# Row ranks spread evenly over the partitions, and each expert's down projection as plain fp32 matmuls

## The chip, the cores and the metric

The kernel runs on one core of one Trainium2 chip. The metric is the device time of one execution in microseconds (us); lower is better. Three runs of the kernel before gave 1128.08, 1129.69 and 1132.62 us; the median is 1129.69 us.

## The reference

One layer of an encoder trunk on two sequences of 512 tokens with 1024 channels, in fp32. Its first two sub-layers (a mix of state-space heads, neighbourhood attention and pooling, then cross attention) are not touched. The third is a mixture of experts: each of the 1024 tokens picks one of four groups and then two of its eight experts, so the 32 experts get 64 rows each on average.

```
def expert_block(args):
    idx, wts, e = args
    xb = x_pad[idx]
    hb = jax.nn.silu(xb @ w_e_gate[e]) * (xb @ w_e_up[e])
    return (hb @ w_e_down[e]).astype(jnp.float32) * wts[:, None]
```

`w_e_gate` and `w_e_up` are 1024x256 for an expert, `w_e_down` is 256x1024, so an expert has three matrices of 1 MiB each.

## The kernel before

**Order of the work.** A written-out list of steps (`timeline()`) orders everything up to the router. Then comes a loop over the 32 experts, which takes the last 370 us or so. Each engine has its own program, and semaphores couple them.

**Splitting in two.** The matrix products are made from fp32 operands split into a high part (an fp32r copy made by ACT) and a low part (the difference, made by DVE). `three` (lines 944 to 948) issues high*high, high*low and low*high as three fp32r matmuls. For the experts `ghi`/`egl` are the parts of the gate and up matrices, `xgH`/`xgL` those of the gathered rows.

**The expert's loop.** SP loads the matrices (`load_piece`, L891) into four buffers each, in the order gate and up of expert n, down of expert n-1; `load_in(n)` waits until expert n-4 has used its buffer (`g_used`), and `load_down` for `d_used`. POOL gathers the rows of an expert by an index list from HBM (`gather_rows`, into `xg`), gathers the partial sums of the same rows (`gather_sums`, into `pg`), and scatters the new sums back (`store_rows`), all with indirect copies of 4 KiB rows; a `gather_sums` waits until an earlier store into its buffer's place has landed (`px_st`). PE does, for n: turn the hidden rows of n-1 (`turn_hidden`), turn the rows of n+1 (`turn_rows`), gate and up of n (`gate_up`), and the down product of n-1 (`down`). ACT does `hidden_high(n-1)`, `rows_high(n+1)`, `gate_high(n+1)`, `hidden_silu(n)`, `down_high(n+1)`; DVE does `hidden_low(n-1)`, `rows_low(n+1)`, `gate_low(n+1)`, `hidden(n)`, `add_rows(n-1)`, `down_low(n+1)`. ACT and DVE take their instructions strictly in that order.

**The down product** contracts over 256 hidden channels, in two chunks k of 128. Before, chunk 0 is done with `three` from split operands (`hbH`, `hbL`, `dhi`, `edl`), chunk 1 as one plain fp32 matmul of `hbF` with the loaded matrix, for each of two halves of 512 columns.

**Where a row sits.** A token has a rank within its expert. `iota_s` holds for each of the 128 partitions the rank that it serves; a one-hot comparison with it (L2089) and a matmul give the list `idh` of the row for each partition. Partition p serves rank p//8 + 16*(p mod 8). Partitions whose rank is beyond the expert's count get an index out of bounds, and the copies skip them.

**The end.** When the first 28 experts' stores have landed, SP copies all partial sums to the outputs (L926, eight copies of 512 KB). Then POOL scatters the rows of the last four experts over them (`out_rows`, L2443).

Of the kernel before, what the change touches and what calls it, by code (L numbers as in the profile page):

```python
# [13 lines left out]
F32 = mybir.dt.float32  # L14
# [5 lines left out]
ALU = mybir.AluOpType  # L20
# [3 lines left out]
P = 128  # L24
# [5 lines left out]
NT = SEQS * TPS  # L30
# [13 lines left out]
NG, EPG, NE = 4, 8, 32  # L44
# [255 lines left out]
def encoder_layer(nc, dram, out):  # L300
# [3 lines left out]
    with ctx:  # L304
        def sem(name):
            return ctx.enter_context(nc.semaphore(name))
# [6 lines left out]
        hb_ps = ctx.enter_context(nc.psum_tensor("hb_ps", [P, 512], F32))  # L313
        r_ps = ctx.enter_context(nc.psum_tensor("r_ps", [P, 512], F32))
        y_ps = ctx.enter_context(nc.psum_tensor("y_ps", [P, 1024], F32))
# [142 lines left out]
        iota_s = sb("iota_s", [P, P])  # L458
# [34 lines left out]
        edr = [se(f"edr{i}", [P, 2, D], b, o) for i, (b, o) in enumerate(d_place)]  # L493
        edl = [se(f"edl{i}", [P, 2, D], b, o, F32R) for i, (b, o) in enumerate(d_place)]
        ghi = [se(f"ghi{i}", [P, 2, KT, DE], "x_sb", 4 * K4 * i, F32R) for i in range(2)]
        dhi = [se("dhi0", [P, 2, D], "Wl1", 0, F32R), se("dhi1", [P, 1, D], "Wl1", K4, F32R)]
# [6 lines left out]
        def sw(name, shape, dt=F32):  # L503
            t = nc.alloc_sbuf_tensor_at(name, shape, dt, offset=small[0])
            small[0] += -(-int(np.prod(shape[1:])) * (2 if dt == BF16 else 4) // 32) * 32
            assert small[0] <= at["router_b"]
            return t
# [2 lines left out]
        ehb = sw("ehb", [P, DE])  # L510
        hbH = sw("hbH", [P, 2, P], F32R)
        hbL = sw("hbL", [P, 2, P], F32R)
        hbF = sw("hbF", [P, P])
        idh = sw("idh", [P, NE], U32)
        idp = sw("idp", [P, NE], U32)
        ids = sw("ids", [P, NE], U32)
# [29 lines left out]
        r_pool = sem("r_pool")  # L546
# [12 lines left out]
        eg_ld = [[sem(f"eg_ld{i}{a}") for a in range(2)] for i in range(4)]  # L559
        ed_ld = [sem(f"ed_ld{i}") for i in range(4)]  # L560
        ghi_done = sem("ghi_done")
        dhi_done = sem("dhi_done")
        glo_done = sem("glo_done")
        dlo_done = sem("dlo_done")
        g_used = sem("g_used")
        d_used = sem("d_used")
        xg_ld = [sem(f"xg_ld{i}") for i in range(3)]
# [5 lines left out]
        hb_done = sem("hb_done")  # L573
        hb_full = sem("hb_full")
        hb_high = sem("hb_high")
        hb_low = sem("hb_low")
        ey_done = sem("ey_done")
        px_st = [sem(f"px_st{i}") for i in range(4)]
        copied = sem("copied")
# [90 lines left out]
        def wait_full(eng, step, j=0):  # L670

            n = plan.place[step, j]
            eng.wait_ge(full[n % N_BANKS], n // N_BANKS + 1)
# [269 lines left out]
        def _(pe):  # L943
            def three(dst, ah, al, bh, bl, first, last):

                pe.matmul(dst, ah, bh, start=first, stop=False)  # L946
                pe.matmul(dst, ah, bl, start=False, stop=False)  # L947
                return pe.matmul(dst, al, bh, start=False, stop=last)  # L948
# [51 lines left out]
            for step in TL:  # L1000
# [5 lines left out]
                if kind == "hT":  # L1006
# [6 lines left out]
                    for half in range(2):  # L1013
                        b = take(pe, step, half)
# [9 lines left out]
                elif kind == "hn3":  # L1024

                    pe.wait_ge(hnorm, 1 + nth(*step))
                    b = take(pe, step)
# [8 lines left out]
                elif kind == "dtt":  # L1036
                    wait_released(pe, ("dtp", step[1]))
                    b = take(pe, step)
# [4 lines left out]
                elif kind == "vt":  # L1043
                    wait_released(pe, ("vc",) + step[1:])
                    b = take(pe, step)
# [265 lines left out]
            def turn_hidden(n):  # L1311

                pe.wait_ge(hb_done, n + 1)
                if n:
                    pe.wait_ge(hb_low, n)
                for k in range(2):
                    last = pe.transpose(hb_ps[:, k * P:(k + 1) * P], ehb[:, k:DE:2], ident[:, :])
                last.then_inc(hb_full, 1)

            def down(n):  # L1320

                pe.wait_ge(hb_low, n + 1)
                pe.wait_ge(dlo_done, n + 1)
                if n:
                    pe.wait_ge(ey_done, n)
                lo = edl[n % 4]
                for half in range(2):
                    c = slice(half * 512, half * 512 + 512)
                    three(y_ps[:, c], hbH[:, 0, :], hbL[:, 0, :], dhi[n % 2][:, 0, c], lo[:, 0, c], True, False)
                    last = pe.matmul(y_ps[:, c], hbF[:, :], edr[n % 4][:, 1, c], start=False, stop=True)  # L1330
                last.then_inc(d_used, 1)

            turn_rows(0)
# [53 lines left out]
        def _(act):  # L1387
# [11 lines left out]
            def copy(dst, src, **kw):  # L1399
                return act.activation(dst, src, ACT.Copy, **kw)  # L1400
# [225 lines left out]
                    copy(xgH[n % 2][:, 4 * half:4 * half + 4, :],  # L1626
                         xg_ps[:, half * 512:half * 512 + 512].rearrange("p (a b) -> p a b", a=4)).then_inc(xg_high, 1)

            def down_high(n):
                act.wait_ge(ed_ld[n % 4], 16 * (n // 4 + 1))  # L1630
                if n > 1:
                    act.wait_ge(d_used, n - 1)
                elif n == 0:
                    wait_full(act, ("xo", NT - 1), 1)
                copy(dhi[n % 2][:, 0, :], edr[n % 4][:, 0, :]).then_inc(dhi_done, 1)

            def hidden_silu(n):
                act.wait_ge(g_used, n + 1)
                if n:
# [3 lines left out]
            def hidden_high(n):  # L1643
                act.wait_ge(hb_full, n + 1)
                if n:
                    act.wait_ge(d_used, n)
                copy(hbF[:, :], hb_ps[:, P:2 * P])
                copy(hbH[:, 0, :], hb_ps[:, 0:P]).then_inc(hb_high, 1)

            down_high(0)  # L1650
            act.wait_ge(ids_done, 1)
            act.wait_ge(g_in, 1)
            act.activation(r_g[:, :, :], r_g[:, :, :], ACT.Exp)
# [3 lines left out]
            gate_high(1, 1)  # L1657
            hidden_silu(0)
            rows_high(1)
            down_high(1)  # L1660
            for n in range(1, NE):
                hidden_high(n - 1)
                if n + 1 < NE:
                    rows_high(n + 1)
                    gate_high(n + 1, 0)
                    gate_high(n + 1, 1)
                hidden_silu(n)
                if n + 1 < NE:
                    down_high(n + 1)
            hidden_high(NE - 1)  # L1670

            def more_first():
                act.wait_ge(g_used, NE)
                act.wait_ge(hb_low, NE)

            def more(b):
                act.wait_ge(d_used, b + NE)
# [15 lines left out]
        def _(dve):  # L1693
# [424 lines left out]
                    tt(xgL[n % 2][:, f, :], xg_ps[:, half * 512:half * 512 + 512].rearrange("p (a b) -> p a b", a=4),  # L2118
                       xgH[n % 2][:, f, :].bitcast(F32), ALU.subtract).then_inc(xg_low, 1)

            def down_low(n):
                dve.wait_ge(dhi_done, n + 1)
                tt(edl[n % 4][:, 0, :], edr[n % 4][:, 0, :], dhi[n % 2][:, 0, :].bitcast(F32), ALU.subtract)\  # L2123
                    .then_inc(dlo_done, 1)

            def hidden(n):
                dve.wait_ge(th_done, n + 1)
                if n:
                    dve.wait_ge(hb_full, n)
                b = gu_ps[n % 2]  # L2130
                tt(ehb[:, :], eth[:, :], b[:, DE:2 * DE], ALU.mult).then_inc(hb_done, 1)

            def hidden_low(n):
                dve.wait_ge(hb_high, n + 1)
                tt(hbL[:, 0, :], hb_ps[:, 0:P], hbH[:, 0, :].bitcast(F32), ALU.subtract).then_inc(hb_low, 1)

            def add_rows(n):
                e = expert(n)
# [52 lines left out]
                dve.tensor_copy(ovi[:, NO:NO + 1], ov[:, 1, NE - 1:NE]).then_inc(count_done, 1)  # L2191

            gate_low(0, 1)
            down_low(0)
            rows_low(0)
            gate_low(1, 0)
            gate_values()
# [1 line left out]
            gate_low(1, 1)  # L2199
            rows_low(1)  # L2200
            slot_values()
            down_low(1)
            for n in range(1, NE):
                hidden_low(n - 1)
                if n + 1 < NE:
                    rows_low(n + 1)
                    gate_low(n + 1, 0)
                    gate_low(n + 1, 1)
                hidden(n)
                add_rows(n - 1)  # L2210
                if n + 1 < NE:
                    down_low(n + 1)
                if n == 2:
                    counts()
                if n == 3:
                    half_rows()
            hidden_low(NE - 1)
            add_rows(NE - 1)

            def more_first():  # L2220
# [65 lines left out]
        def _(pool):  # L2286
# [25 lines left out]
            for step in TL:  # L2312
# [7 lines left out]
                elif kind == "gain":  # L2320
# [5 lines left out]
                    if step[1] == "ffn":  # L2326
                        pool.memset(router_w[:, :, NG:8], 0.0)
                        pool.memset(router_b[:, NG:8], NEG).then_inc(r_pool, 1)
                        pool.iota(iota_e[:, :], [[1, NE]], base=0, channel_multiplier=0,
                                  allow_small_or_imprecise_dtypes=True).then_inc(r_pool, 1)  # L2330
                        pool.iota(iota_p[:, :], [[1, P]], base=0, channel_multiplier=0,
                                  allow_small_or_imprecise_dtypes=True).then_inc(r_pool, 1)
                        pool.iota(iota_s[:, :].rearrange("p (a b) -> p a b", a=16), [[1, 16], [16, 8]], base=0,
                                  channel_multiplier=0, allow_small_or_imprecise_dtypes=True).then_inc(r_pool, 1)
                        pool.iota(token0[:, :], [[P, NT]], base=0, channel_multiplier=1,
                                  allow_small_or_imprecise_dtypes=True).then_inc(r_pool, 1)
                        pool.iota(token1[:, :], [[P, NT]], base=1, channel_multiplier=1,
                                  allow_small_or_imprecise_dtypes=True).then_inc(r_pool, 1)
                        parts = (("w_router_group", "b_router_group", 0, NG), ("w_router_expert", "b_router_expert", 8, NE))
                        for w, b_, o, m in parts:  # L2340
                            pool.dma_start(router_w[:, :, o:o + m], dram[w][0].rearrange("(k p) n -> p k n", p=P))\
                                .then_inc(router_ld, 16)
                            pool.dma_start(router_b[:, o:o + m], bass.AP(dram[b_].tensor, 0, [[0, P], [1, m]]))\
                                .then_inc(router_ld, 16)
# [232 lines left out]
```

## Time and profile before

| | |
|---|---|
| median of three runs | 1129.69 us |
| the profiled execution, its own time | 1130.85 us |
| its span in the profile | 1129.0 us |
| PE busy over the span | 1002.6 us (89%) |
| DVE / ACT / POOL busy | 774.9 / 474.0 / 299.7 us |
| moved by DMA in all | 197.41 MB |
| mean granted TensorE clock | 0.948 |

The profile shows one execution. A window's row gives its bounds and length, the busy time of PE, of PE's weight loads, DVE, ACT and POOL in it (with the number of instructions), then the granted clock of TensorE (1.00 is full speed), the mean busy share of the core's 16 DMA engines, and the rate they moved. A matmul's duration includes its fill and drain, which overlap with the next matmul; the chain of waits counts only the time by which each one moved the chain on. "L1330" is line 1330 of the kernel.

### The profile page before, as it was taken

The page shows a single profiled execution, that of the slowest core. Times are in us where ns is not written, and L with a number is a line of the kernel's source. Part 1 is how long each engine was busy: PE and PEld are TensorE (multiplying, and loading weights), DVE is VectorE, ACT ScalarE, POOL GpSimd, SP SyncE. Part 2 cuts the span into 40 slices and gives each one's busy share as a digit, 9 for nine tenths or more (in the row PEclk, how much of TensorE's full clock was granted, in tenths as well). Part 3 has the DMA queues.
Part 4 walks back from the last instruction along what each step waited for, and adds up shares of the span by engine and source line. Part 5 has one row for each costly group of instructions (what it writes and reads, how often), then busy time and mean ns, then how long its engine had stood idle before and what let it go on. Part 6 is the DMA issues. An engine that isn't in the chain of part 4 may idle for free.

```text
span 1129.0 us, 13999 instructions
## 1 busy us (share of the span) xinstructions
PE 1002.6 (89%) x5029; PEld 801.8 (71%) x5029; DVE 774.9 (69%) x1241; ACT 474.0 (42%) x860; POOL 299.7 (27%) x347
## 2 busy tenths in 40 slices
PE   5998988998989899999979999849999988888892
PEld 4776767776768678788868888737777766666671
DVE  5557677776777577862455777668988877787771
ACT  5144442233455234322233343325666655555540
POOL 2234132312521422100110212023354332323122
PEclk9999998997999989899989999958999999999996
DMA  7222242111223514424120112937999999999872
GB/s 237 84 85 94 66 142 76 57 56 56 94 75 98 163 58 136 129 71 178 56 63 19 57 57 109 376 135 272 360 363 369 378 362 342 362 336 368 329 251 74
DMA packets 63396, 197.41 MB, mean 175 GB/s; under 512 B 16416, under 2 KB 22976, under 8 KB 50912
## 3 DMA queue, kind: packets, MB, share of 16 engines
q1 hardware_dynamic: 43344, 152.73, 37.4%
q0 software_dynamic: 18688, 39.52, 10.0%
q10 hardware_dynamic: 1296, 4.26, 0.9%
q8 instruction: 41, 0.67, 0.2%
q14 instruction: 27, 0.22, 0.1%
HBM read 190.17 MB, written 37.75 MB: 202 GB/s over the span
## 4 chain that ended last, share of the span: by engine, by line
PE 51%; DMA 18%; DVE 13%; issue 9%; ACT 4%; POOL 3%; SPq 0%; ACTq 0%; POOLq 0%; DVEq 0%
PE bank L946 10%; PE bank L947 9%; PE bank L948 9%; DMA partial_rows<-pg,idh 9%; DMA edr<-w_e_down 4%; PE gu_ps L946 2%; PE gu_ps L948 2%; PE gu_ps L947 2%; PE bank L1017 2%; PE bank L1135 2%; PE y_ps L1330 2%; DMA pg<-partial_rows,idh 2%; DVE egl L1740 1%; DVE Wl L1758 1%; ACT dec L1585 1%
## 5 line engine op out<-in xcount | busy, mean ns | idle before, releaser
L946 PE MATMUL bank<-Wh,hTh 128*128 128x512 f32 x384 | 156.6, 408 | 1.2 <-DVE hTl L1782 1.2
L1740 DVE TENSOR_TENSOR egl<-egr,ghi 128x2048 fp32r<-128x2048 f32 x64 | 143.9, 2288 | 15.0 <-ACT ghi L1400 15.0
L947 PE MATMUL bank<-Wl,hTh 128*128 128x512 f32 x384 | 152.1, 396 | 0.0
L948 PE MATMUL bank<-Wh,hTl 128*128 128x512 f32 x384 | 151.6, 395 | 0.0
L1400 ACT ACTIVATE ghi<-egr 128x2048 fp32r<-128x2048 f32 x64 | 119.6, 1931 | 0.0
L946 PE MATMUL gu_ps<-ghi,xgH 128*128 128x512 f32 x256 | 104.0, 406 | 1.4 <-DVE xgL L2118 1.4
L948 PE MATMUL gu_ps<-ghi,xgL 128*128 128x512 f32 x256 | 101.2, 395 | 0.0
L947 PE MATMUL gu_ps<-egl,xgH 128*128 128x512 f32 x256 | 100.9, 394 | 0.0
L946 PEld LDWEIGHTS bank<-Wh,hTh 128*128 128x128 f32 x384 | 74.0, 193 | 17.8 <-issue 1.6
L1400 ACT ACTIVATE dhi<-edr 128x1024 fp32r<-128x1024 f32 x32 | 33.9, 1060 | 122.9 <-DMA edr<-w_e_down 93.2
L948 PEld LDWEIGHTS bank<-Wh,hTl 128*128 128x128 f32 x384 | 73.6, 192 | 16.2
L947 PEld LDWEIGHTS bank<-Wl,hTh 128*128 128x128 f32 x384 | 73.9, 193 | 14.6
L2438 POOL DMA_INDIRECT pg<-partial_rows,idh x32 | 43.2, 1351 | 146.0 <-DMA partial_rows<-pg,idh 142.9
L946 PE MATMUL bank<-hTh,Wh 128*128 128x512 f32 (+1 forms) x176 | 73.3, 416 | 1.1 <-DVE x_sb L1818 0.8
L947 PE MATMUL bank<-hTl,Wh 128*128 128x512 f32 (+1 forms) x176 | 70.9, 403 | 0.0
L948 PE MATMUL bank<-hTh,Wl 128*128 128x512 f32 (+1 forms) x176 | 70.6, 401 | 0.0
L1330 PE MATMUL y_ps<-edr,hbF 128*128 128x512 f32 x128 | 65.4, 592 | 0.0
L2123 DVE TENSOR_TENSOR edl<-edr,dhi 128x1024 fp32r<-128x1024 f32 x32 | 39.1, 1221 | 38.3 <-ACT dhi L1400 38.3
L1758 DVE TENSOR_TENSOR Wl<-raw,Wh 128x1024 fp32r<-128x1024 f32 (+1 forms) x45 | 55.0, 1228 | 12.3 <-ACT Wh L1400 12.3
L2297 POOL TENSOR_SCALAR ms<-ssq 128x1 f32<-128x1 f32 x28 | 6.4, 230 | 212.0 <-ACT xn_ffn L1460 96.8
L1585 ACT ACTIVATE dec<-dec,ncs 128x128 f32<-128x128 f32 x128 | 38.3, 388 | 50.8 <-DVE dec L1961 50.8
L946 PEld LDWEIGHTS gu_ps<-ghi,xgH 128*128 128x128 f32 x256 | 49.1, 192 | 11.0 <-DVE xgL L2118 1.8
(326 smaller groups left out, 2231.7 us busy)
## 6 DMA issues: line engine op xcount, KB each, us to landing
egr<-w_e_gate SPq DMA_DIRECT2D x32, 1024.0 KB
egr<-w_e_up SPq DMA_DIRECT2D x32, 1024.0 KB
edr<-w_e_down SPq DMA_DIRECT2D x32, 1024.0 KB
raw<-w_in SPq DMA_DIRECT2D x50, 256.0 KB, 3.0
xn<-w_in SPq DMA_DIRECT2D x22, 256.0 KB, 3.0
x_sb<-x_prompt SPq DMA_DIRECT2D x8, 512.0 KB, 6.5
partial_rows<-x_sb ACTq DMA_DIRECT2D x8, 512.0 KB, 2.6
ffn_rows<-xn_ffn POOLq DMA_DIRECT2D x8, 512.0 KB, 3.0
```

The costliest lines, as they stand in the source:

```text
L946: pe.matmul(dst, ah, bh, start=first, stop=False)
L947: pe.matmul(dst, ah, bl, start=False, stop=False)
L948: return pe.matmul(dst, al, bh, start=False, stop=last)
L1017: last = pe.transpose(b[:, j * P:(j + 1) * P], src[:, f * P:(f + 1) * P], ident[:, :])
L1135: last = pe.matmul(b[:, hc], dec[:, dr, h, :], xdt[:, dr, hc], start=dr == 0, stop=dr == 1)
L1330: last = pe.matmul(y_ps[:, c], hbF[:, :], edr[n % 4][:, 1, c], start=False, stop=True)
L1400: return act.activation(dst, src, ACT.Copy, **kw)
L1585: last = act.activation(dec[:, dr, h, :], dec[:, dr, h, :], ACT.Exp, bias=ncs[:, dr, c, h:h + 1])
L1740: tt(egl[n % 4][:, a, :, :], egr[n % 4][:, a, :, :], ghi[n % 2][:, a, :, :].bitcast(F32), ALU.subtract)\
L1758: tt(lo, src, h, ALU.subtract).then_inc(w_low, 1)
L2123: tt(edl[n % 4][:, 0, :], edr[n % 4][:, 0, :], dhi[n % 2][:, 0, :].bitcast(F32), ALU.subtract)\
L2438: return pool.indirect_dma_start(out=to, out_offset=None, in_=table, in_offset=bass.IndirectOffsetOnAxis(ap=idx, axis=0), bounds_check=bou ...
```

## The change

Two things. First, `iota_s` gets another pattern: partition p = 16a + 8b + 4c + d serves rank 2a + 16b + c + 32d (a below 8, b and c below 2, d below 4). Second, both chunks of the down product become plain fp32 matmuls of the loaded matrix with the hidden rows; the split of the down matrix (`down_high` on ACT, `down_low` on DVE) and the low part of the hidden rows (`hidden_low` on DVE) go, and one ACT copy of 256 columns takes the place of two of 128. PE waits directly for the load of the down matrix.

```diff
-        hbF = sw("hbF", [P, P])
+        hbF = sw("hbF", [P, 2, P])
...
             def down(n):
-                pe.wait_ge(hb_low, n + 1)
-                pe.wait_ge(dlo_done, n + 1)
+                pe.wait_ge(hb_high, n + 1)
+                pe.wait_ge(ed_ld[n % 4], 16 * (n // 4 + 1))
                 if n:
                     pe.wait_ge(ey_done, n)
-                lo = edl[n % 4]
                 for half in range(2):
                     c = slice(half * 512, half * 512 + 512)
-                    three(y_ps[:, c], hbH[:, 0, :], hbL[:, 0, :], dhi[n % 2][:, 0, c], lo[:, 0, c], True, False)
-                    last = pe.matmul(y_ps[:, c], hbF[:, :], edr[n % 4][:, 1, c], start=False, stop=True)
+                    for k in range(2):
+                        last = pe.matmul(y_ps[:, c], hbF[:, k, :], edr[n % 4][:, k, c], start=k == 0, stop=k == 1)
...
-            def down_high(n):
-                act.wait_ge(ed_ld[n % 4], 16 * (n // 4 + 1))
-                if n > 1:
-                    act.wait_ge(d_used, n - 1)
-                elif n == 0:
-                    wait_full(act, ("xo", NT - 1), 1)
-                copy(dhi[n % 2][:, 0, :], edr[n % 4][:, 0, :]).then_inc(dhi_done, 1)
...
-                copy(hbF[:, :], hb_ps[:, P:2 * P])
-                copy(hbH[:, 0, :], hb_ps[:, 0:P]).then_inc(hb_high, 1)
+                copy(hbF[:, :, :], hb_ps[:, 0:2 * P].rearrange("p (a b) -> p a b", a=2)).then_inc(hb_high, 1)
...
-            def down_low(n):
-                dve.wait_ge(dhi_done, n + 1)
-                tt(edl[n % 4][:, 0, :], edr[n % 4][:, 0, :], dhi[n % 2][:, 0, :].bitcast(F32), ALU.subtract)\
-                    .then_inc(dlo_done, 1)
...
-            def hidden_low(n):
-                dve.wait_ge(hb_high, n + 1)
-                tt(hbL[:, 0, :], hb_ps[:, 0:P], hbH[:, 0, :].bitcast(F32), ALU.subtract).then_inc(hb_low, 1)
...
-                        pool.iota(iota_s[:, :].rearrange("p (a b) -> p a b", a=16), [[1, 16], [16, 8]], base=0,
-                                  channel_multiplier=0, allow_small_or_imprecise_dtypes=True).then_inc(r_pool, 1)
+                        pool.iota(iota_s[:, :].rearrange("p (a b c d) -> p a b c d", a=8, b=2, c=2),
+                                  [[2, 8], [16, 2], [1, 2], [32, 4]], base=0, channel_multiplier=0, allow_small_or_imprecise_dtypes=True).then_inc(r_pool, 1)
```

The calls of the removed functions go too, and waits on `hb_low` elsewhere become waits on `hb_high` or `d_used`.

## Rows read from the trace of the kernel before

**Rows 1.** Windows: PE, PEld, DVE, ACT, POOL busy, clock, DMA share, GB/s

```profile
784.00:889.00 105.00, 104.49 (x476) 80.98 (x475) 93.50 (x97) 69.66 (x87) 48.64 (x31) 1.00 0.97 372
900.00:1080.00 180.00, 158.67 (x701) 118.28 (x700) 138.03 (x129) 99.60 (x129) 53.39 (x46) 1.00 0.91 347
```

**Rows 2.** Timeline of SP's queue: loads issued as gate_up of an expert ends

```profile
781.58 0.33 SPq L891 DMA_DIRECT2D egr<-w_e_gate  x1
...
821.24 0.33 SPq L891 DMA_DIRECT2D egr<-w_e_gate  x1
...
889.28 0.33 SPq L891 DMA_DIRECT2D egr<-w_e_gate  x1
...
899.02 0.33 SPq L891 DMA_DIRECT2D egr<-w_e_gate  x1
...
1057.16 0.33 SPq L891 DMA_DIRECT2D egr<-w_e_gate  x1
```

**Rows 3.** Waits between 760 and 1080 us: total, times, longest in us

```profile
POOL pg L2438 <- DMA partial_rows<-pg,idh: 130.0, 20, 8.2
ACT dhi L1400 <- DMA edr<-w_e_down: 88.3, 18, 5.6
```

**Rows 4.** The chain that ended last, around one down product

```profile
1057.12 0.23 PE y_ps L946
...
1057.82 0.86 PE y_ps L1330 x2
...
1059.38 0.87 PE y_ps L1330 x2
1060.27 25.60 DMA edr<-w_e_down
```

**Rows 5.** Windows in which DMA carries little but indirect row copies

```profile
761.00:762.00 1.00, 0.90 (x2) 0.80 (x3) 0.05 (x1) 1.00 (x1) 0.70 (x2) 0.50 0.58 213
...
766.00:767.00 1.00, 1.00 (x5) 0.86 (x4) 0.90 (x4) 0.00 (x0) 0.00 (x0) 0.86 0.48 70
```

**Rows 6.** Windows: a plain store of 128 rows alone, and matrix loads alone

```profile
646.00:647.00 1.00, 1.00 (x11) 0.96 (x9) 0.71 (x3) 0.00 (x0) 0.00 (x0) 1.00 0.97 401
...
718.00:722.00 4.00, 4.00 (x33) 3.66 (x31) 3.72 (x15) 0.38 (x3) 0.79 (x3) 1.00 1.03 432
```

**Rows 7.** Groups of instructions by form, 720 to 1129 us

```profile
L1330 PE MATMUL y_ps<-edr,hbF 128*128 128x512 f32 x128 | 65.4, 592 | 0.0
...
L2123 DVE TENSOR_TENSOR edl<-edr,dhi 128x1024 fp32r<-128x1024 f32 x32 | 39.1, 1221 | 38.3 <-ACT dhi L1400 38.3
L1400 ACT ACTIVATE dhi<-edr 128x1024 fp32r<-128x1024 f32 x32 | 33.9, 1060 | 122.9 <-DMA edr<-w_e_down 93.2 <-PE y_ps L1330 29.7
...
L1641 ACT ACTIVATE eth<-gu_ps 128x256 f32<-128x256 f32 x32 | 12.6, 393 | 17.4 <-PE gu_ps L948 17.4
```

**Rows 8.** Timeline: POOL around the table, and an indirect copy beside another

```profile
560.61 0.37 POOL L2333 IOTA iota_s<- 128x128 f32 x1
...
760.60 1.00 POOL L2438 DMA_INDIRECT pg<-partial_rows,idh  x1 [0.31 <-issue]
...
761.90 1.00 POOL L2438 DMA_INDIRECT pg<-partial_rows,idh  x1 [0.30 <-issue]
```

**Rows 9.** Timeline of the end

```profile
1073.15 1.28 DVE L2143 SCALAR_TENSOR_TENSOR pg<-y_ps,gate_s,pg 128x1024 f32<-128x1024 f32 x1
...
1090.01 2.50 SPq L926 DMA_DIRECT2D y_prompt<-partial_rows  x4
...
1100.98 0.38 ACT L1641 ACTIVATE eth<-gu_ps 128x256 f32<-128x256 f32 x1 [5.02 <-PE gu_ps L948]
...
1107.17 1.01 POOL L2443 DMA_INDIRECT y_prompt<-pg,idp  x1 [13.90 <-issue]
...
1109.05 1.28 DVE L2143 SCALAR_TENSOR_TENSOR pg<-y_ps,gate_s,pg 128x1024 f32<-128x1024 f32 x1 [3.48 <-PE y_ps L1330]
...
1114.89 0.97 POOL L2443 DMA_INDIRECT y_prompt<-pg,idp  x1 [0.30 <-issue]
```

More of the change, by code:

```diff
@@ L561, in encoder_layer @@
         ghi_done = sem("ghi_done")
-        dhi_done = sem("dhi_done")
         glo_done = sem("glo_done")
-        dlo_done = sem("dlo_done")
         g_used = sem("g_used")
@@ L575, in encoder_layer @@
         hb_high = sem("hb_high")
-        hb_low = sem("hb_low")
         ey_done = sem("ey_done")
@@ L1314, in turn_hidden @@
                 if n:
-                    pe.wait_ge(hb_low, n)
+                    pe.wait_ge(hb_high, n)
                 for k in range(2):
@@ L1646, in hidden_high @@
                     act.wait_ge(d_used, n)
-                copy(hbF[:, :], hb_ps[:, P:2 * P])
-                copy(hbH[:, 0, :], hb_ps[:, 0:P]).then_inc(hb_high, 1)
-            down_high(0)
+                copy(hbF[:, :, :], hb_ps[:, 0:2 * P].rearrange("p (a b) -> p a b", a=2)).then_inc(hb_high, 1)
             act.wait_ge(ids_done, 1)
@@ L1659, in _ @@
             rows_high(1)
-            down_high(1)
             for n in range(1, NE):
@@ L1667, in _ @@
                 hidden_silu(n)
-                if n + 1 < NE:
-                    down_high(n + 1)
             hidden_high(NE - 1)
@@ L1673, in more_first @@
                 act.wait_ge(g_used, NE)
-                act.wait_ge(hb_low, NE)
+                act.wait_ge(d_used, NE)
             def more(b):
@@ L2193, in _ @@
             gate_low(0, 1)
-            down_low(0)
             rows_low(0)
@@ L2201, in _ @@
             slot_values()
-            down_low(1)
             for n in range(1, NE):
-                hidden_low(n - 1)
                 if n + 1 < NE:
@@ L2210, in _ @@
                 add_rows(n - 1)
-                if n + 1 < NE:
-                    down_low(n + 1)
                 if n == 2:
@@ L2216, in _ @@
                     half_rows()
-            hidden_low(NE - 1)
             add_rows(NE - 1)
```

## The prediction

> **What bounds the kernel now.** I read the windows by stage first, then SP's queue, the waits and the chain. The change touches only the expert loop, so everything before 781 us stays (the table itself is one instruction on POOL of 0.37 us at 560 us [rows 8], far from its use).
>
> The loop has two halves. Until 889 us PE is busy 104.5 of 105 us; from 900 to 1080 us it is busy 158.7 of 180 us, with the DMA engines busy 0.91 of the time at 347 GB/s [rows 1]. SP's queue gives the pace, since it issues a gate matrix whenever the product gate_up of an expert ends: the rows at 781.58 and 821.24 us are experts 1 and 5, those at 889.28, 899.02 and 1057.16 us experts 12, 13 and 27. From 821.24 to 889.28 us that is 68.04/7 = 9.72 us an expert; from 899.02 to 1057.16 us it is 158.14/14 = 11.30 us [rows 2]. So PE paces the first twelve experts and DMA the rest: PE at first lives on the matrices loaded ahead. Drawn backwards at 11.30 us an expert from 899.02 us, DMA's line stands at 763.4 us for expert 1, which is 18.2 us ahead of PE's 781.58; that is the lead. The waits agree: ACT stands 88.3 us for down matrices and POOL 130.0 us for stores of partial sums to land [rows 3], and the chain goes through a down load of 25.60 us [rows 4].
>
> **Why DMA needs 11.30 us.** An expert moves 3 x 1 MiB of matrices and 3 x 64 rows of 4 KiB (rows in, sums in, sums out), 3.15 + 0.79 = 3.93 MB; 347 GB/s x 11.30 us = 3.92 MB agrees. But when DMA has little but indirect row copies, it stands at a share of 0.48 to 0.58 and at most some 210 GB/s [rows 5], while a plain store of 128 rows of the same size reaches 0.97 and 401 GB/s, and matrices alone 432 GB/s [rows 6]. The old table puts ranks 0 to 63 on the partitions with p mod 8 below 4: four used, four unused, all along. I read this as: the DMA engines serve fixed small blocks of partitions, and half of them get nearly all rows. Check: the loaded half carries 3.15/16 + 0.79/8 = 0.295 MB per engine and expert; at one engine's rate of 383/16 = 23.9 GB/s (372 at 0.97 [rows 1] is 383 at full share) to 432/16 = 27.0 GB/s that is 12.3 to 10.9 us, which brackets 11.30. Against it: were all rows on eight engines, the mean share would be (1 + 0.197/0.295)/2 = 0.83, not 0.91, so some rows (ranks above 63) lie on the others.
>
> **The table.** With the new one, ranks 0 to 63 take two partitions in every block of four, so every engine carries 0.246 MB: 10.3 us at 23.9 GB/s, 9.1 us at 27.0. The share gives the same upper end: 0.91 x 11.30 = 10.3 us. I take 10.2, near the mixed row. It costs nothing.
>
> **The down product on PE.** One chunk split in three moves the chain by 0.23 us three times, 0.69 us (one of three rows stands), one plain fp32 chunk (two instructions) by 0.86 to 0.87 [rows 4]. For both halves: before 2 x (0.69 + 0.865) = 3.11 us, after 4 x 0.865 = 3.46. So PE pays 0.35 us more for each expert, and its pace becomes 10.07 us. The lower bound is that the saved changes between kinds of matmul give the 0.35 back (9.72); the upper takes the mean duration of one L1330 instruction, 592 ns [rows 7], as if none overlapped: 8 x 0.592 = 4.74 us, a pace of 11.35. I take 0.865 because it is the distance of starts in the chain, while 592 ns contains the wait behind the neighbour.
>
> The page "FP8 and Floating Point Precision" of the Trainium skill, section TensorE Precision Notes, has true fp32 as four passes through the array. Four times the 0.23 us of an fp32r pass [rows 4] would be 0.92, where the row has 0.865; by the rule the down product would be 3.68 us and the pace 10.29 us, 7 us more over the loop.
>
> **ACT and DVE.** ACT loses 1.06 us (dhi) an expert, and for two copies of 128 columns it gets one of 256, 0.39 us by the silu of that width. DVE loses the 1.22 us of edl [rows 7] and the small subtraction for hbL. While PE paces, both are partly hidden already (DVE 93.5 of 105 us, ACT 69.7 [rows 1]); I count nothing for them. They hide behind PE's 10.07 us, DVE had 93.5/105 x 9.72 = 8.7 us of work in it and has less now. What does count is the place of a wait. ACT stood at `down_high(n+1)` for a down load, with `hidden_high(n)`, `rows_high(n+2)` and `gate_high(n+2)` queued behind it, although gate and up of n+2 had been loaded before that down matrix. Now PE waits for the down matrix of n only after gate_up of n+1, one expert later. Where DMA paces, the gate split starts up to one load earlier: 1.05 MB at 347 GB/s = 3 us, once, plus the 1.06 us. Where PE paces, nothing. POOL: its `gather_sums` waits for stores, and behind it are queued `store_rows` and `gather_rows`; with half the rows per loaded engine those land sooner, and nothing new is waited for.
>
> **The sum.** PE's line: expert 1 at 781.6 us, 30 experts x 10.07 = 302.1, less 0.9 for the last one, which turns no rows: the last gate_up ends at 1082.8 instead of 1100.98 us [rows 9]. DMA's line: 763.4 + 30 x 10.2 = 1069.4 us, 13 us ahead, so PE paces to the end; DMA would take over only above 10.64 us an expert. That is -18.2 us at the last gate_up.
>
> The end has two paths [rows 9]. PE's: down of 30, turn, copy, down of 31 and the addition end 9.4 us later (before 9.35: 1110.33 - 1100.98), at 1092.2; the last scatters start no earlier, and from the one at 1114.89 to the span's end at 1129.0 are 14.1 us: 1106.3. The stores': the addition for expert 27 ended at 1074.43 us, 54.6 us before the end (15.6 until the stores had landed and SP copied at 1090.01, 17.2 for the copies, 21.8 for scatters and landing). Now it ends at 781.6 + 27 x 10.07 + 4.7 = 1058.2, so the span ends at 1112.8 if stores land as slowly as before, and at 1106.3 (PE's path) if they land in half the time. I take 1111. This path is the likelier, since the copies follow the slowest store. The profiled execution took 1.85 us more than its span and 1.16 more than the median, so the median becomes 1111 + 1.85 - 1.16 = 1111.7, say 1112.
>
> **Rivals.**
> (B) DMA gains only part and paces the last experts. For it: mixed windows never show more than 383 GB/s at full share. Against: rows and matrices alone both exceed 400. At 10.95 us an expert its line ends at 763.4 + 328.5 = 1091.9 us, 9 us behind PE's line; less up to 4 us for the earlier split: 1117 to 1121. The page "DMA: Bandwidth & Descriptors" of the Trainium skill, section Where 436 GB/s comes from, says that for HBM traffic a limit of some 358 GB/s per core binds. By that, 3.93 MB would take 10.97 us and this rival would come true at its slow end. Matrices alone at 432 GB/s [rows 6] speak against the rule here, so it gets a small part of this case.
> (C) The table does nothing. The half share of the indirect copies may be POOL's pace: one copy each 1.30 us [rows 8], and 64 rows in 1.30 us are 202 GB/s, just what the windows show. Against: after the last of them the engines still work on at 0.48 [rows 5], and 11.30 us fits the loaded half. Then DMA keeps 11.30 us, its line ends where it does now, only the earlier down wait gives 0 to 4 us: 1125 to 1130.
> (D) Slower: plain fp32 costs PE what the 592 ns say. Pace 11.35 us: the last gate_up at 781.6 + 340.5 - 0.9 = 1121.2 us, 20 us late: 1150. It decides from the point where PE's pace passes 10.68 us, that is 0.51 us an instruction instead of 0.43; there the last gate_up ends where it does now. The chain's rows speak against it.
>
> **Chances.** Forecast 0.60 (1106 to 1117); B 0.17; C 0.15; D 0.05; faster still, below 1105, 0.03. A measurement of this kernel can tell about 0.5% from no change, 5.6 us: faster means below 1124.0, slower above 1135.3. So faster 0.60 + 0.17 + 0.03 = 0.80, same 0.14 of C, slower D with the rest, 0.06. Range: 1105 to 1124 leaves out C, D and the fastest tail, 0.2.
>
> **What would show it.** Right: loads of gate matrices in SP's queue every 10.07 us up to the last expert, PE busy near 100% to the end of the loop, DMA at 385 to 395 GB/s, copies of rows alone at a share near 1.0, eight L1330 instructions taking 3.46 us in a row, and stores landing within some 10 us. Wrong: a pace above 10.7 us late in the loop with PE idle (B, C); row copies alone still at a share of 0.55 (C); L1330 instructions starting 0.5 us or more apart (D). The prediction also fails if DMA's share was held up by something other than the rows.

## The result, and the profile after

The changed kernel takes 1104.86 us (median of four runs, 1101.08 to 1105.81) against 1130.38 us for the kernel before: a ratio of 0.9768, with a 95% interval of 0.9737 to 0.9799. It is faster by about 25.5 us, where 18 were forecast; the forecast of 1112 us was 7 us too slow, and the measured median lies 0.14 us below the stated range. The profiled execution is the fastest of the four, 1101.08 us with a span of 1099.3 us. It came to the list of rows (`idh`) 4.1 us earlier than the profiled one of before, at 748.56 instead of 752.68 us, before any line of the change matters. Its own time stands 3.8 us below the median, and the span difference of 29.7 us flatters the change.

Windows of the changed kernel, in the columns of [rows 1]:

```profile
784.00:889.00 105.00, 105.00 (x438) 74.10 (x437) 78.24 (x74) 55.34 (x62) 46.71 (x30) 1.00 0.99 381
889.00:1000.00 111.00, 111.00 (x468) 79.19 (x467) 81.85 (x67) 60.38 (x67) 50.34 (x33) 1.00 1.00 395
```

PE is busy every microsecond in both; before, it was idle for 21 of the 180 us in the second stretch [rows 1]. The DMA engines move 395 GB/s where they moved 347. DVE has 78.2 us of work where it had 93.5.

SP's queue, as in [rows 2]: each row is the end of gate_up of an expert, here 1, 2, 26 and 27.

```profile
774.41 0.33 SPq L888 DMA_DIRECT2D egr<-w_e_gate  x1
...
784.46 0.33 SPq L888 DMA_DIRECT2D egr<-w_e_gate  x1
...
1025.63 0.33 SPq L888 DMA_DIRECT2D egr<-w_e_gate  x1
...
1035.68 0.33 SPq L888 DMA_DIRECT2D egr<-w_e_gate  x1
```

The first and last are 26 experts apart: 261.27/26 = 10.05 us, and the pairs at both ends have the same 10.05. There is no second half any more. The down product is one piece of the chain:

```profile
1055.74 3.43 PE y_ps L1326 x8
```

Eight instructions in 3.43 us, 0.43 each, although the group of L1326 still gives a mean of 592 ns. The waits between 760 and 1060 us have turned round. Of the two waits of [rows 3], that of 130.0 us has shrunk to 1.7 us and that of 88.3 us is gone:

```profile
POOL partial_rows L2411 <- DVE pg L2117: 145.2, 28, 9.3
ACT hbF L1396 <- PE hb_ps L1314: 95.4, 30, 3.3
...
POOL pg L2406 <- DMA partial_rows<-pg,idh: 1.7, 1, 1.7
```

POOL and ACT now wait for what PE drives, no longer for DMA. The stretch before the loop, where DMA carries little but row copies (compare [rows 5]):

```profile
755.00:756.00 1.00, 0.00 (x0) 0.00 (x0) 0.80 (x2) 1.00 (x2) 0.82 (x1) 0.50 0.74 246
756.00:757.00 1.00, 0.98 (x2) 0.83 (x3) 0.00 (x0) 1.00 (x2) 0.69 (x2) 0.50 0.76 246
757.00:758.00 1.00, 1.00 (x4) 0.77 (x3) 0.91 (x1) 1.00 (x2) 0.69 (x2) 0.50 0.77 242
...
759.00:760.00 1.00, 1.00 (x5) 0.77 (x5) 0.90 (x5) 1.00 (x1) 1.00 (x1) 0.83 0.64 242
```

In the first three rows the share is 0.74 to 0.77, well above the 0.48 to 0.58 of before, but not the 1.0 that the prediction wanted to see.

And the end, as in [rows 9]:

```profile
1054.89 2.50 SPq L923 DMA_DIRECT2D y_prompt<-partial_rows  x4
```

```profile
1071.89 1.01 POOL L2411 DMA_INDIRECT y_prompt<-pg,idp  x1 [13.69 <-issue]
...
1079.98 0.97 POOL L2411 DMA_INDIRECT y_prompt<-pg,idp  x1 [3.22 <-DVE pg L2117]
...
1085.12 0.97 POOL L2411 DMA_INDIRECT y_prompt<-pg,idp  x1 [2.89 <-DVE pg L2117]
```

The addition for expert 27 ended at 1050.45 us, and SP could copy 4.4 us later instead of 15.6. POOL's last two pairs of scatters waited for DVE's additions, that is for PE's last products. Before, all eight went out one behind the other, since the stores had been late.

### The profile page after: what moved, and what is told of

Its sections match the earlier page's. It is cut to its first block, busy times and chain, and to the rows that moved or that the text cites. A ratio compares the mean times of both kernels' runs of the same rounds, so it can differ in the third digit from the quotient of the medians.

```text
span 1099.3 us, 13712 instructions
## 1 busy us (share of the span) xinstructions
PE 1003.5 (91%) x4965; PEld 787.2 (72%) x4965; DVE 734.9 (67%) x1177; ACT 446.7 (41%) x796; POOL 315.4 (29%) x347
## 4 chain that ended last, share of the span: by engine, by line
PE 69%; DVE 12%; issue 8%; ACT 3%; POOL 3%; DMA 2%; SPq 0%; ACTq 0%; POOLq 0%; DVEq 0%
PE bank L943 10%; PE bank L944 10%; PE bank L945 10%; PE y_ps L1326 9%; PE gu_ps L943 5%; PE gu_ps L945 5%; PE gu_ps L944 5%; PE xg_ps L1292 3%; PE bank L1014 2%; PE bank L1132 2%; DVE Wl L1741 1%; ACT dec L1581 1%; PE bank L1219 1%; PE bank L1263 1%; PE bank L1187 1%
## 5 line engine op out<-in xcount | busy, mean ns | idle before, releaser
L1326 PE MATMUL y_ps<-edr,hbF 128*128 128x512 f32 x256 | 115.1, 592 | 1.2 <-DVE pg L2117 1.2
L1326 PEld LDWEIGHTS y_ps<-edr,hbF 128*128 128x128 f32 x256 | 48.5, 190 | 49.9 <-issue 45.9
L2406 POOL DMA_INDIRECT pg<-partial_rows,idh x32 | 75.4, 2356 | 11.2 <-issue 9.5
L2117 DVE SCALAR_TENSOR_TENSOR pg<-y_ps,gate_s,pg 128x1024 f32<-128x1024 f32 x32 | 41.1, 1284 | 53.4 <-PE y_ps L1326 51.8
L2411 POOL DMA_INDIRECT partial_rows<-pg,idh x28 | 28.3, 1009 | 145.2 <-DVE pg L2117 145.2
## 6 DMA issues: line engine op xcount, KB each, us to landing
egr<-w_e_up SPq DMA_DIRECT2D x32, 1024.0 KB, 10.2
edr<-w_e_down SPq DMA_DIRECT2D x32, 1024.0 KB, 10.2
```

Source lines behind the costliest of these rows:

```text
L1326: last = pe.matmul(y_ps[:, c], hbF[:, k, :], edr[n % 4][:, k, c], start=k == 0, stop=k == 1)
L2117: stt(pg[n % 4][:, :], y_ps[:, :], gate_s[:, e:e + 1], pg[n % 4][:, :], ALU.mult, ALU.add)\
L2406: return pool.indirect_dma_start(out=to, out_offset=None, in_=table, in_offset=bass.IndirectOffsetOnAxis(ap=idx, axis=0), bounds_check=bou ...
L2411: return pool.indirect_dma_start(out=table, out_offset=bass.IndirectOffsetOnAxis(ap=idx, axis=0), in_=frm, in_offset=None, bounds_check=bo ...
```

## The experiments

The kernel before was measured anew beside them, at 1129.21 us for e1 to e4 and 1130.68 us for e5, e6, e8 and e9; each ratio is to its own one of these.

**One part alone.** The first kernel is the kernel before with the new table only; the second is the changed kernel with the old table.

```diff
 e1 (on the kernel before), the reverse for e2 (on the changed kernel):
-  pool.iota(iota_s[:, :].rearrange("p (a b) -> p a b", a=16), [[1, 16], [16, 8]], ...)
+  pool.iota(iota_s[:, :].rearrange("p (a b c d) -> p a b c d", a=8, b=2, c=2),
+            [[2, 8], [16, 2], [1, 2], [32, 4]], ...)
```

> The kernel before with the new rank table alone; the down product stays split. Theory (the table frees DMA, the plain down product costs PE 0.35 us an expert): PE paces to the end at 9.72 us an expert instead of 10.05, DMA follows at about 9.95 us (3.93 MB at 395 GB/s) within its lead of some 18 us; time 1130 - 26 - 10 = 1094 us. Rival 1 (ACT's wait for the down matrix, which stays here, holds up the gate split as soon as DMA is near its limit): pace above 10 us late in the loop, ACT again idle for tens of us before L1400 dhi, time 1100 to 1108. Rival 2 (the gain came from the down product, not from the table): about 1130.

Measured: 1094.17 us (1092.93 to 1095.71), a ratio to the kernel before of 0.9682 (0.9661 to 0.9704). That is the theory's number. The loop runs at 9.72 us an expert to the end, but for one step of 10.51 us after gate_up of expert 3 that the kernel before has too; SP's rows of experts 1, 2 and 27:

```profile
778.59 0.33 SPq L891 DMA_DIRECT2D egr<-w_e_gate  x1
...
788.31 0.33 SPq L891 DMA_DIRECT2D egr<-w_e_gate  x1
...
1032.12 0.33 SPq L891 DMA_DIRECT2D egr<-w_e_gate  x1
```

ACT's wait for the down load is harmless as soon as DMA keeps up: in this run's list of waits `dhi` waits 80.8 us for PE's down products, and no wait for a down load appears among the longest. Rivals 1 and 2 fall. The table alone beats the whole change by 10.7 us in the medians (1104.86 - 1094.17). Against the kernel before of its own series it saves 35.0 us where the whole change saves 25.5, which makes 9.5; the profiled executions differ by 9.5 too, from the list of rows to the end (550.7 and 541.2 us).

> The changed kernel with the old rank table. Theory: DMA paces the late experts at 11.2 to 11.3 us again, since half of its engines carry the rows; only the later wait for the down matrix helps, once and by 0 to 4 us: 1125 to 1130 us, PE idle in the second half, indirect copies alone at a DMA share of 0.5 to 0.6. Rival (fewer ACT and DVE instructions and the later wait are what freed the loop): pace of 10.05 us to the end and about 1105 us.

Measured: 1129.41 us (1127.22 to 1132.47), ratio 1.0004 (0.9989 to 1.0020). The down product gives nothing by itself, as forecast. But the loop is not what it was. Gate_up of experts 1 and 19 end at 779.56 and 960.44 us, 10.05 us an expert, and only then comes DMA's pace, 11.3 us on average (970.91 us for expert 20, 1072.38 us for expert 29). The last gate_up ends at 1092.44 instead of 1100.98 us, and still the end does not move, because the stores set it:

```profile
1088.46 2.50 SPq L923 DMA_DIRECT2D y_prompt<-partial_rows  x4
```

This is only 1.6 us earlier than in the kernel before [rows 9], 18.3 us after the addition for expert 27. The path of the stores, not PE's, ends the kernel here as it does before.

**Which partitions share an engine.** Two more tables tell two readings apart.

```diff
 e3 (on the kernel before, in place of the old pattern):
+  pool.iota(iota_s[:, :].rearrange("p (a b c d) -> p a b c d", a=2, b=2, c=8),
+            [[8, 2], [64, 2], [1, 8], [16, 4]], ...)
 e4 (on the changed kernel, in place of the new pattern):
+  pool.iota(iota_s[:, :], [[1, P]], ...)
```

> The kernel before with a third table: ranks 0 to 15 each in another group of partitions, rank r at partition 64*(r mod 16 // 8) + 4*(r mod 8) + r//16 (plus 28 from rank 64 on), so ranks 0 to 63 fill the partitions 0 to 31 and 64 to 95. Theory A (an engine serves a block of four partitions and the block 32 further on, and the upper 64 partitions have other engines): all engines are loaded evenly, as e1 or 0 to 2 us less: 1092 to 1094 us. Theory B (an engine serves every sixteenth block of four, so blocks 64 partitions apart share one): ranks 0 to 63 lie on half the engines again, and it ends like before, about 1130 us.

Measured: 1094.27 us (1093.28 to 1096.06), ratio 0.9691 (0.9668 to 0.9715).

> The changed kernel with rank r at partition r, so ranks 0 to 63 fill partitions 0 to 63. Theory A of e3: half of the engines carry nearly all rows, as with the old table: 1122 to 1130 us and a pace of 11.2 us late in the loop. Theory B: all 16 engines are loaded evenly, about 1105 us. A third reading (any dense packing is as good as the new table, only the old one's gaps hurt): 1105 us as well.

Measured: 1136.15 us (1134.99 to 1139.10), ratio 1.0057 (1.0040 to 1.0075). Both go with theory A and against B. Partitions 0 to 63 alone are half of the engines; 0 to 31 with 64 to 95 are all of them. The page "DMA: Bandwidth & Descriptors" of the Trainium skill, section The descriptor swizzle, gives for a plain transfer to 128 partitions the engine as 8*(partition >> 6) + ((partition >> 2) & 7). The old table, the new one, e3 and e4 all come out as that rule would have it for indirect copies.

The traces' records of single packets show the halves more directly. Take the five microseconds from 0.5 us after the first gather into `pg`, when little but rows is under way. Exactly eight packets of 4 KiB are in flight, as eight busy engines would have it, for 37% of that time in the kernel before and 34% in e4, but for 5% in the changed kernel and in e3. Twelve or more are in flight for 30% and 27% against 59% and 63%.

The straight table was expected at 1122 to 1130 us and is 6 us worse than that, and 6.7 us worse than e2. By the same rule an expert with 48 rows would put eight rows on some engines and four on others with the straight table, and six on each of its eight engines with the old one; that this is the reason was argued, not tried.

**What DMA can do by itself.** With the change PE paces the loop, so its trace can't show DMA's own limit. Three kernels take work from PE: they leave out the product of the rows' high part with the low part of the gate and up matrices.

```diff
 gate_up, in e5 (new table), e6 (old table) and e9 (table of e3):
-                    last = three(gu_ps[n % 2]..., xgH, xgL, hi, lo, k == 0, k == KT - 1)
...
+                    pe.matmul(g, xgH[n % 2][:, k, :], hi[:, :, k, :], start=k == 0, stop=False)
+                    last = pe.matmul(g, xgL[n % 2][:, k, :], hi[:, :, k, :], start=False, stop=k == KT - 1)
```

> The changed kernel (new table) with the low part of the gate and up matrices left out of gate_up: two matmuls for each k instead of three, so PE needs 8 x 0.227 = 1.8 us less for an expert (10.05 to 8.23 us) and is no longer what paces the loop. It leaves out one of the three products of gate and up. Theory: DMA paces at what 3.93 MB take at 395 GB/s, 9.9 to 10.0 us an expert, at a share of 1.00. Rival (DMA has more to give, the 395 GB/s in the changed kernel were only PE's demand): 9.2 to 9.5 us. In both cases the stage cannot go below DVE's 7.5 us.

Measured: 1087.16 us (two runs, 1087.05 and 1087.28), ratio 0.9614 (0.9594 to 0.9635). Not what was expected at first: experts 2 to 22 run at 8.85 us, not paced by DMA, since the lead lasts that long (and not at 8.23, so something beside PE's work holds it, which was not looked into). Then gate_up of experts 22 and 30 end at 962.65 and 1041.86 us: 9.90 us an expert, the theory's number. The two ends, and DMA in a stretch that holds the end of the lead and the start of its own pace:

```profile
962.65 0.38 ACT L1630 ACTIVATE eth<-gu_ps 128x256 f32<-128x256 f32 x1
...
1041.86 0.38 ACT L1630 ACTIVATE eth<-gu_ps 128x256 f32<-128x256 f32 x1
```

```profile
880.00:1000.00 120.00, 111.02 (x446) 72.94 (x445) 93.42 (x77) 69.95 (x79) 55.22 (x37) 1.00 1.02 419
```

> As e5, with the old table: the same product left out. Theory: DMA's own pace with half of its engines carrying the rows, 11.2 to 11.4 us an expert from the first experts on, at a share of 0.91 to 0.92; the loop ends where DMA's line ends in the kernel before, 1120 to 1130 us. Rival (PE's work also slows the DMA side of the kernel before): clearly below 11 us.

Measured: 1126.89 us (1125.55 to 1130.17), ratio 0.9969 (0.9955 to 0.9983). From expert 10 (859.37 us) to expert 30 (1083.61 us) the pace is 11.21 us. The late pace holds; "from the first experts on" does not, the lead carries nine experts here. Taking 1.8 us of PE's work out of each expert leaves the kernel with the old table 0.3% below the kernel before: DMA was the bound, whatever PE did.

```profile
880.00:1000.00 120.00, 97.47 (x359) 62.41 (x357) 77.26 (x64) 57.55 (x64) 50.39 (x33) 0.94 0.91 350
```

> As e5, with the table of e3, which spreads every 16 ranks over 16 groups of partitions where the new table needs 32 ranks for an even spread: the same product left out. Theory: the most loaded engine carries up to one row less of each copy, some 0.15 us each and 0.2 to 0.4 us an expert: 9.6 to 9.8 us. Rival (the limit is the sum over all engines, not the most loaded one): the same as e5 to 0.1 us.

Measured: 1080.63 us (two runs, 1080.13 and 1081.12), ratio 0.9557 (0.9535 to 0.9578), 6.5 us faster than e5. In the profiled executions 4.6 us of it lie between the list of rows and the last gate_up (294.5 against 299.2 us). At the end of its lead, from expert 25 (988.42 us) to expert 30 (1036.48 us), the pace is 9.61 us. With this table every 16 ranks are spread over all engines, so no engine gets two rows more than another. That fits the theory that the most loaded engine counts and not the sum over all, which would have left the pace at 9.9; the 9.61 rest on five experts of one execution.

**The place of the wait.** In e2 the last gate_up ended 8.5 us early where the prediction gave the later wait 0 to 4 us.

```diff
 e8 (on e2), ACT's loop:
                 hidden_silu(n)
+                if n + 1 < NE:
+                    act.wait_ge(ed_ld[(n + 1) % 4], 16 * ((n + 1) // 4 + 1))
```

> The kernel of e2 (old table, plain down product) with only the old wait put back: ACT waits for the down matrix of expert n+1 after the silu of n, without copying it. In e2 the last gate_up ended at 1092.4 us, 8.5 us before that of the kernel before, where 0 to 4 us were expected of the later wait. Theory (the place of the wait makes this): the last gate_up ends at 1098 to 1101 us. Rival (the removed copy and subtraction make it): it stays at 1092 to 1094 us. The whole time is set by the stores of partial sums and moves by less than half of that: 1129 to 1133 us.

Measured: 1129.21 us, ratio 0.9987 (0.9974 to 1.0000), and the wait is back:

```profile
ACT hbF L1396 <- DMA edr<-w_e_down: 84.5, 15, 7.5
```

DMA's pace sets in after expert 14, as it did after expert 13 in the kernel before and after expert 19 in e2. The last gate_up ends at 1096.14 us, between theory and rival. The three executions came to the list of rows at different times, so the distance from there is fairer: 348.3 us in the kernel before, 346.2 here, 341.8 in e2. So of 6.5 us the wait's place makes 4.4; the rest is the removed work, or differences between single executions. None of it reaches the end.

## Why the prediction was nearly right

**What bounds the kernel: right.** Rows on half of the engines, a lead used up by PE, then DMA's pace. e2 and e6 show 11.3 and 11.2 us with the old table, with PE's whole load and with less, e5 9.90 with the new one, where the prediction's term was 10.2 (9.1 to 10.3).

**PE's price: right.** 0.35 us an expert, measured 10.05 - 9.72 = 0.33, and some 10 us in all between e1 and the changed kernel. The 592 ns of a single instruction, on which rival D stood, were overlap. The page "FP8 and Floating Point Precision" of the Trainium skill, section TensorE Precision Notes, has four passes for true fp32, from which the prediction estimated 3.68 us for the product. The row is 3.43 us, so the estimate is 7% too high.

**ACT and DVE at nothing: right** for the time. Together with PE's price this makes the down part of the change a loss of some 10 us where PE paces, hidden in a change that gains 25. With the old table it costs nothing (e2).

**Why 7 us too slow.** Two terms were mis-sized. The first is the step "The change touches only the expert loop, so everything before 781 us stays". The distance from the list of rows to the end of gate_up of expert 1 is 28.90 us in the kernel before, 28.88 in e2, 28.93 in e4 and 29.5 in e8 (tables on half of the engines), but 25.86 in the changed kernel, 25.86 in e1 and 25.97 in e3: 3.0 us, and it goes with the table, not with the down product. One microsecond is PE's wait for the first gathered rows, 4.71 us instead of 5.67. The rest comes with TensorE's clock, in two parts. In the changed kernel the granted clock rose from 1.2 to 2.4 GHz at 759.3 us (the 0.83 in the row from 759 us shown above), 3.3 us into gate_up of expert 0; in the kernel before at 766.3 us, 5.2 us into it. That product took 7.3 us instead of 8.2. In all ten traces this rise comes 10.5 to 10.8 us after the list of rows with an even table and 13.5 to 14.5 us after it with the others. The other part comes one expert later. Windows of the kernel before and, below, of the changed one, each around the turning of expert 2's rows:

```profile
773.00:778.00 5.00, 4.34 (x18) 3.91 (x19) 3.78 (x8) 2.96 (x4) 1.18 (x2) 0.66 1.03 430
```

```profile
764.00:768.00 4.00, 1.48 (x23) 1.30 (x23) 3.96 (x6) 1.27 (x3) 2.80 (x1) 1.00 0.86 317
768.00:774.00 6.00, 6.00 (x32) 5.06 (x32) 4.03 (x5) 4.70 (x4) 1.00 (x1) 1.00 0.98 405
```

In both PE waits 2.52 us for DVE before it turns these rows. In the kernel before, the granted clock then fell for part of the stretch to its lower level of 1.2 GHz; in the changed one it stayed at 2.4. That makes gate_up of expert 1 end 11.06 instead of 12.30 us after that of expert 0. The table as such does not decide this part. The clock fell here in every kernel with a table on half of the engines (e6 too, 0.50 from 774.0 to 777.4 us), but also in e5 and e9, whose table is even: there gate_up of expert 1 ends 13.2 us after that of expert 0, although it has less work. What decides it stays open.

The second is the end. The prediction said of the two paths "This path is the likelier, since the copies follow the slowest store" and took 28.2 us from the last gate_up to the end of the span. The stores were ready to copy after 4.4 us, not after 7.8 to 15.6, so PE's path ended the kernel: 24.3 us, where the prediction's own sum for it gave 23.5. That is 3.9 us. From the list of rows to the end of the span the prediction has 558.3 us (1111 - 752.68) and the profiled execution 550.7 (1099.3 - 748.56). Of these 7.6 us, 3.0 are the start, 3.9 the end and 0.6 PE's pace (300.6 us for the last 30 experts instead of 301.2). Between the medians it is 6.8 us, 1111.7 against 1104.86.

The prediction let the stores' delay follow from the rows per engine ("with half the rows per loaded engine those land sooner"), and that step is not borne out. From the addition for expert 27 to the copies it takes 4.4 us in the changed kernel, 4.4 in e3 and 7.7 in e1, where PE paces. It takes 15.2 us in e5 and 14.8 in e9, whose rows are spread as evenly, and 15.6 to 19.7 us in the kernel before, e2, e4, e6 and e8; in all of these DMA paces late. So a short delay goes with DMA not being what the loop waits for.

**Rivals.** B did not come true: DMA at 0.99 to 1.00 share keeps PE's pace. The page "DMA: Bandwidth & Descriptors" of the Trainium skill, section Where 436 GB/s comes from, has HBM traffic bound at some 358 GB/s, by which DMA could not have kept up. The runs, on one core alone, do not agree: 395 GB/s here and 419 in e5. C fell with e1. But its reading of the row copies was half right: they run alone at 242 to 246 GB/s and a share of 0.77 even with an even table. POOL's 1.30 us a copy may be the limit there, which was not tried; the window was a poorer witness for the half load than the prediction made it. The proof is in e3, e4 and the packets in flight, not in the share of that window.

## What to carry to other kernels

Indirect row copies that fill only part of the partitions load DMA engines by where the rows sit. All four tables here fit blocks of four partitions, with p and p+32 on the same engine. Spread the used ranks over those blocks, every 16 of them if you can, before taking work from compute engines. And time the parts of a change one by one: here one part gained 35 us and the other gave some 10 of them back.

## What the runs showed that was not expected

- A table that fills partitions densely from 0 is worse than one with gaps, 1136.15 against 1129.41 us, although both put ranks 0 to 63 on half of the engines.
- The time between the addition for expert 27 and the copies fell from 15.6 to 4.4 us, but not by the even table alone: e5 and e9 have it and take 15.2 and 14.8 us, with DMA pacing.
- After the same wait of 2.52 us on PE the granted clock fell in the kernel before, e2, e4 and e8 and stayed up in the changed kernel, e1 and e3; between the kernel before and the changed one that is 1.2 us.
